# Order of the small matmuls in a retention chunk and in the token mixing of a hybrid decoder layer

## The reference

```
# A, per chunk c and head h:
mixed = einsum('hij,bcjhd->bcihd', tril(w), vn)

# C, per chunk of 128 positions, S the state of each head (64 x 64):
sc = einsum('bihd,bjhd->bhij', qc, kc) * dmask
o  = einsum('bhij,bjhe->bihe', sc, vc) + einsum('bihd,bhde->bihe', qc * q_dec, S)
S  = chunk_dec * S + einsum('bjhd,bjhe->bhde', kc * k_dec, vc)
```

## Time and profile before

| | |
|---|---|
| runs | 1394.23, 1397.78 and 1398.0 us, median 1397.78 |
| profiled execution, first to last instruction | 1397.8 us |
| TensorE matmuls busy | 1359.0 us, 97% |
| VectorE busy | 713.3 us, 51% |
| ScalarE busy | 454.8 us, 33% |
| GpSimd busy | 36.3 us, 3% |
| L660, probabilities times v | 128 instructions, median 273 ns |
| L663, query times state | 96 instructions, median 294 ns |
| L731, token mixing | 64 instructions, median 273 ns |

### The profile page before, as it was taken

The page is one execution under the profiler, slowest core; times in us unless marked ns, Lnnn a source line. Parts: engine busy times, 40 slices in busy tenths (PEclk is TensorE's granted clock), DMA queues, the critical chain, the costliest instruction groups (busy, mean ns, idle before and its releaser), DMA issues.

```text
span 1397.8 us, 25646 instructions
## 1 busy us (share of the span) xinstructions
PE 1359.0 (97%) x10681; PEld 1312.8 (94%) x10681; DVE 713.3 (51%) x887; ACT 454.8 (33%) x630; POOL 36.3 (3%) x60
## 2 busy tenths in 40 slices
PE   7999999989999999999979999999999999999997
PEld 6999888989999999999879998899999999999996
DVE  6856658386344444222377465765944444442225
ACT  4532124454222222222254511244522222232222
POOL 3000002000000000000020000020000000000000
PEclk9999998999999999999989999999999999999999
DMA  6323112213332233222343221132222322222221
GB/s 217 91 76 89 49 46 81 91 54 98 90 90 78 87 90 90 83 87 66 110 122 89 76 78 46 46 101 86 64 88 90 90 86 80 89 90 83 91 84 64
DMA packets 110473, 119.09 MB, mean 85 GB/s; under 512 B 4576, under 2 KB 107128, under 8 KB 110136
## 3 DMA queue, kind: packets, MB, share of 16 engines
q1 hardware_dynamic: 107456, 108.57, 25.6%
q0 software_dynamic: 2496, 8.27, 2.0%
q10 hardware_dynamic: 440, 1.09, 0.2%
HBM read 113.23 MB, written 4.69 MB: 84 GB/s over the span
## 4 chain that ended last, share of the span: by engine, by line
PE 89%; DVE 5%; ACT 3%; issue 2%; DMA 0%; ACTq 0%; DVEq 0%
PE ps L491 27%; PE ps L493 27%; PE ps L492 26%; PE ps L660 1%; DVE x L1168 1%; PE ps L663 1%; ACT h_hi L911 1%; DVE r_post L1152 1%; PE ps L703 1%; PE ps L678 1%; PE ps L521 1%; DVE y L1163 1%; PE ps L641 1%; DVE r_pre L1205 1%; PE ps L719 1%
## 5 line engine op out<-in xcount | busy, mean ns | idle before, releaser
L491 PE MATMUL ps<-h_hi,w_hi 128*128 128x272 f32 x2240 | 661.7, 295 | 21.3 <-DVE h_lo L1189 11.2
L493 PE MATMUL ps<-h_lo,w_hi 128*128 128x272 f32 x2240 | 649.3, 290 | 0.0
L492 PE MATMUL ps<-h_hi,w_lo 128*128 128x272 f32 x2240 | 647.1, 289 | 0.0
L491 PEld LDWEIGHTS ps<-h_hi,w_hi 128*128 128x128 f32 x2240 | 425.1, 190 | 32.0 <-ACT h_hi L911 22.6
L492 PEld LDWEIGHTS ps<-h_hi,w_lo 128*128 128x128 f32 x2240 | 427.3, 191 | 2.9 <-issue 2.5
L493 PEld LDWEIGHTS ps<-h_lo,w_hi 128*128 128x128 f32 x2240 | 424.3, 189 | 0.0
L1132 DVE TENSOR_TENSOR w_lo<-w_raw,w_hi 128x1024 fp32r<-128x1024 f32 (+1 forms) x208 | 244.9, 1182 | 276.2 <-ACT w_hi L892 274.2
L892 ACT ACTIVATE w_hi<-w_raw 128x1024 fp32r<-128x1024 f32 (+1 forms) x208 | 211.7, 1021 | 234.8 <-DMA w_raw<-in_w_down 146.0
L491 PE MATMUL ps<-f_hi,w_hi 128*128 128x272 f32 x704 | 204.2, 290 | 0.0
L493 PE MATMUL ps<-f_lo,w_hi 128*128 128x272 f32 x704 | 203.1, 289 | 0.0
L492 PE MATMUL ps<-f_hi,w_lo 128*128 128x272 f32 x704 | 202.4, 288 | 0.0
(11 more groups left out here) (177 smaller groups left out, 1141.2 us busy)
## 6 DMA issues: line engine op xcount, KB each, us to landing
w_raw<-in_w_in SPq DMA_DIRECT2D x52, 512.0 KB, 3.7
w_raw<-in_w_gate SPq DMA_DIRECT2D x44, 512.0 KB, 3.7
w_raw<-in_w_up SPq DMA_DIRECT2D x44, 512.0 KB, 3.7
w_raw<-in_w_down SPq DMA_DIRECT2D x36, 512.0 KB, 3.4
w_raw<-in_w_out SPq DMA_DIRECT2D x16, 512.0 KB, 3.4
w_raw<-in_w_down SPq DMA_DIRECT2D x16, 256.0 KB, 2.9
tab<-in_table POOLq DMA_DIRECT2D x2, 1536.0 KB, 6.4
st_s<-in_state_ret POOLq DMA_DIRECT2D x8, 256.0 KB, 4.7
```

Of the source, the lines that this page charges most:

```text
L491: pe.matmul(out, wh, hi[:, cols(half)], start=begins, stop=False)
L492: pe.matmul(out, wl, hi[:, cols(half)], start=False, stop=False)
L493: mm = pe.matmul(out, wh, lo[:, cols(half)], start=False, stop=ends)
```

## The change

In attend, the eight heads' L660 are now issued one after the other, and then, in chunks 1 to 3, the eight heads' query times state in a loop of its own. Since all heads of a half share bank 6, only the first head of each half (heads 0 and 1) now carries the start flag, which marks the bank as unwritten for its partitions. In mix_tokens the two loops change places: for each chunk the four heads, where there were the four chunks for each head.

```
                         out = ps[rows, 6, P * (h // 2):P * (h // 2) + P]
                         pe.matmul(out, v_tok[:, c, HD * h:HD * h + HD], probs[:, c % 2, by_parity(h), :],
-                                  start=True, stop=(c == 0))
-                        if c:
-                            pe.matmul(out, st_p[rows, h // 2, :], qd[rows, h // 2, :], start=False, stop=True)
+                                  start=(h < 2), stop=(c == 0), skip_group_check=True)
+                    for h in range(HEADS) if c else ():
+                        rows = slice(HD * (h % 2), HD * (h % 2) + HD)
+                        out = ps[rows, 6, P * (h // 2):P * (h // 2) + P]
+                        pe.matmul(out, st_p[rows, h // 2, :], qd[rows, h // 2, :], start=False, stop=True,
+                                  skip_group_check=True)
...
                     after(probs_made, 2)
                     after(vn_made, 2)
-                    for h in range(AHEADS):
-                        for c in range(NC):
+                    for c in range(NC):
+                        for h in range(AHEADS):
                             mm = pe.matmul(ps[HD * (h % 2):HD * (h % 2) + HD, 4 + h // 2, P * c:P * c + P],
                                            vn[:, c, HD * h:HD * h + HD], ws_t[:, h, :], start=True, stop=True)
                     task_done(mm)
```

## The result

The changed kernel takes 1373.69 us (median of 4 runs, 1373.1 to 1375.89) against 1397.51 us of the kernel before on the same chip, 23.8 us less. The ratio of the two times is 0.9839, with a 95% interval of 0.9825 to 0.9853. The prediction was 1374.2 us, 23.6 us less. The profiled execution's span went from 1397.8 to 1372.2 us.

What follows compares the result with a forecast made beforehand. TensorE was taken to bound the kernel, busy for all 81.00 us of the stage in each layer. Chunk steps 22.4 us plus token mixing 1.2 make 23.6 us off 1397.8, giving 1374.2 us; range 1369 to 1378.

Steps and rivals of the forecast that it cites:

- TensorE bounds the stage, so its time is the kernel's: First retention chunk to end of sample rows: TensorE busy for all 81.00 us per layer; a microsecond saved there shortens the kernel.
- The change of shape costs, not the second write: Attend, chunks 1 to 3: the 0.36 us steps come from changing array shape, not from accumulating onto one place.
- The terms: Attend, per chunk: L660 0.82, change 0.20, L663 0.82, change to L666 0.20; 2.04 us for 5.77, 22.4 us saved over six.
- Token mixing: L731's 32 instructions per layer: alternating halves save 0.60 us per layer, 1.2 us in all; bound: nothing.
- The lower bound: L663 in chunks 1 to 3 at the pace of L666, 0.41 us to the last start; 24.8 us saved for 22.4.
- The unseen price, L663 at L660's pace: Chunks 1 to 3: eight heads of L663 in a row, shown by no row, taken at 0.82 us to the last start.
- one at a time: Rival for L663 in attend: row tiles take turns at bank 6; saves 17.1 + 1.2 us, 1379.5 us; chance 0.09.
- an empty array after each head: Rival for L663 in attend: array empties after every head, 3.90 us per chunk; saves 11.2 + 1.2, 1385.4 us; chance 0.05.
- The cover: VectorE's idle before chunks 1 and 3 end, 5.10 and 4.00 us, shrinks by 3.73 to 1.37 and 0.27; VectorE is not late.
- The clock: Granted clock full through the chunk stage; half-clock stretches during the sample attention may shift, 1.4 us per layer either way, 2.8 together.
- the slower rival: Clock falls in the chunk stage too, from chunk 1 to the sample attention: 35 us, 1409 us; chance 0.03.

## Why the prediction was right

- *TensorE bounds the stage, so its time is the kernel's.* It stayed so; the 11.8 us that TensorE saved per layer between chunk 0 and the sample attention came out of the time in full. That the total came within 0.2 us (23.8 for 23.6) is more than these runs can tell, and in so far luck: the interval is 20.5 to 24.5 us.
- *The change of shape costs, not the second write.* It was argued from one step, L663 of a head to L660 of the next. The runs with one shape in the old order (1.79 us per chunk) and with alternating shapes at a distance (3.76) show it from both sides. That the array has to be empty first, as the prediction put it, stays an argument; shown is that loads and matmuls of the next shape start 0.20 us behind the last matmul of the one before.
- *The terms:* 0.82 + 0.20 + 0.82 + 0.20 = 2.04 us against 2.04 measured; 5.77 - 2.04 = 3.73, six times. Token mixing 0.60 us per layer against 0.61. The lower bound's 0.61 us for L666 rests on a row that the earlier trace rows doesn't show: L641 starts at 161.39, 0.62 us behind it.
- *The unseen price, L663 at L660's pace,* held: 1.02 us from its first instruction to the state update, where one at a time would have given 2.9 us per chunk and an empty array after each head 3.9. Here two row tiles that write opposite partition halves of one bank run side by side. The Trainium skill says under "Gotcha 1: PSUM Pressure" of TensorEngine Tiling (Array Packing) that different row tiles can't access one PSUM bank at the same time; the measurement differs, and it decides. Under "Key Properties" the same page of the Trainium skill says that changing the tiling mode drains TensorE. The trace agrees that the next shape waits, 0.20 us from the last start of one shape to the first of the next.
- *The cover:* idle of 1.37 and 0.27 us left was forecast, and 1.38 and 0.26 us are there.
- *The clock* stayed full in the chunk stage, so the slower rival had no ground. How long it falls after that was right as an uncertainty: 6.8 us in both layers in the profiled execution, and 3.4 to 10.2 us per layer in the profiles of the six experiments that leave the sample attention as it was.

## What to carry to other kernels

A TensorE that shows as busy may be waiting between its own matmuls: compare start to start, and look for alternating shapes. Issue small matmuls of one shape together, with neighbours in opposite halves of the array; where a product can be padded with zeros to its neighbour's shape at no cost elsewhere, even the two changes left go (1.79 us per chunk for 2.04). Before taking time from one engine, subtract it from the idle time of those that follow: 0.26 us was left here, and the next saving in the sample attention made VectorE the bound.

## What the runs showed of the hardware that was not expected

A product that adds to the place which its head's product just before has written costs no more than any other (0.056 us per instruction in the kernel with one shape in the old order). At a change of shape the weight load waits as well as the matmul, 0.20 us behind the last matmul's start; within a shape the load starts 0.10 us ahead of its matmul. During the sample attention, with 64 matmuls of 8 columns per layer all on one half, the granted clock fell to half in both layers of the kernels before and after (for 6.8 or 10.2 us) while TensorE showed as busy. With the halves alternating and all of it done in 2.55 us, layer 1 kept the full clock, and the fall in layer 0 was 3.4 us. With padded states besides, in both kernels that have them, neither layer shows a fall there. One kernel with the sample attention as it was (alternating shapes at a distance) fell for 3.4 us alone in layer 1, so lengths from single executions overlap. Since the kernels with alternating halves run more matmuls side by side and their sample attention is also shorter, the runs don't tell which of the two keeps the clock up.
